# Latent attention: the first down projection blocks are loaded into other slots of the weight buffer

## The reference

```python
def mla_shared_kv(x, kv_in_g, w_dkv, kv_norm_g, w_uk, w_uv, cos, sin):
    ckv = rmsnorm(x, kv_in_g) @ w_dkv                       # 1024 -> 256 latent + 64 for the rotation
    latent = rmsnorm(ckv[..., :KV_LORA], kv_norm_g)
    k_rope = apply_rope(ckv[..., KV_LORA:], cos, sin)
    k_nope = (latent @ w_uk).reshape(b, s_len, MLA_HEADS, MLA_NOPE)
    v = (latent @ w_uv).reshape(b, s_len, MLA_HEADS, MLA_V)
    return k_nope, k_rope, v

# in mla_mixer: the query goes 1024 -> 768 -> 16 heads
q = (rmsnorm(h @ w_dq, q_norm_g) @ w_uq).reshape(b, s_len, MLA_HEADS, MLA_NOPE + MLA_ROPE)
```

## Time and profile before

| | |
|---|---|
| median of 3 executions | 3567.14 us |
| the three | 3567.11, 3567.14, 3570.8 us |
| profiled execution, its own time | 3568.08 us |
| its span | 3566.1 us |
| mean granted TensorE clock | 0.89 of full |
| PE busy | 2822.0 us, 79% |
| stretch from the end of the first feed-forward to the first scores | 3100.2 to 3175.0 us |

### The profile page before, as it was taken

One profiled execution on the slowest core, in us unless ns is written; L12 is line 12 of the kernel. 1 busy time (PEld: TensorE's weight loads), 2 busy tenths in 40 slices (PEclk: granted clock), 3 DMA queues, 4 the chain that ended last, 5 costly groups with the idle time before them and its releaser, 6 DMA issues.

```text
span 3566.1 us, 53144 instructions
## 1 busy us (share of the span) xinstructions
PE 2822.0 (79%) x19152; PEld 1680.4 (47%) x19152; DVE 2225.3 (62%) x5084; ACT 1393.8 (39%) x3587; POOL 854.8 (24%) x780
## 2 busy tenths in 40 slices
PE   4988898777776877786575977777767989999998
PEld 3877344233222433341144722222115879877997
DVE  5855766768777666678735467777763246523276
ACT  1213444434433334443334243334433247523275
POOL 0001433334343333433400133344440000000000
PEclk8988999999888998886677999999768999999999
DMA  8888999999999999999967699999994235433353
GB/s 328 309 313 347 419 420 420 420 420 408 421 420 394 420 414 415 413 412 387 361 224 257 256 421 421 421 414 421 416 413 159 112 124 194 156 118 109 118 192 127
DMA packets 177293, 1153.12 MB, mean 323 GB/s; under 512 B 21892, under 2 KB 30492, under 8 KB 43436
## 3 DMA queue, kind: packets, MB, share of 16 engines
q0 software_dynamic: 111632, 810.60, 55.4%
q1 hardware_dynamic: 59244, 321.94, 24.1%
q10 hardware_dynamic: 6192, 17.67, 1.3%
HBM read 1128.86 MB, written 21.27 MB: 323 GB/s over the span
## 4 chain that ended last, share of the span: by engine, by line
PE 40%; DMA 37%; DVE 11%; issue 6%; ACT 5%; POOL 1%; SPq 1%; ACTq 0%; DVEq 0%; POOLq 0%
DMA AR<-in_peer_uv,AR 32%; PE PS L2829 10%; PE PS L1308 6%; DVE AR L1496 4%; DMA W<-in_ada_w 3%; PE PS L1266 2%; PE PS L660 2%; PE PS L3327 2%; DVE AR L1471 2%; PE PS L2642 2%; PE PS L390 2%; PE PS L2060 2%; POOL AR L1520 1%; PE PS L521 1%; PE PS L1924 1%
## 5 line engine op out<-in xcount | busy, mean ns | idle before, releaser
L1308 PE MATMUL PS<-AR 64*64 64x512 f32 x6144 | 984.3, 720 | 498.7 <-ACT AR L1382 497.3
L1496 DVE CUSTOM_DVE_ANT_0 AR<-AR,H 128x1024 f32<-128x1024 f32 x768 | 938.4, 1224 | 540.8 <-DMA AR<-in_peer_uv,AR 534.6
L1520 POOL DMA_INDIRECT AR<-in_peer_uv,AR x768 | 850.1, 1107 | 1615.1 <-PE PS L1308 1156.8
L1308 PEld LDWEIGHTS PS<-AR 64*64 64x64 f32 x6144 | 180.1, 148 | 945.3 <-ACT AR L1382 830.0
L1377 ACT ACTIVATE SM<-SM 128x1 f32<-128x1 f32 x768 | 155.5, 202 | 1171.1 <-DVE SM L1496 1170.3
L1266 PE MATMUL PS<-HT,W 128*128 128x256 f32 x1280 | 427.8, 440 | 0.0
L1266 PEld LDWEIGHTS PS<-HT,W 128*128 128x128 f32 x1280 | 217.4, 200 | 424.7 <-issue 413.0
L1382 ACT ACTIVATE AR<-AR,SM 128x64 f32<-128x64 f32 x768 | 267.2, 348 | 25.2
L2829 PE MATMUL PS<-XP,WP 128*128 128x256 f32 x2112 | 258.4, 284 | 6.4 <-ACT AR L3003 3.5
L2829 PEld LDWEIGHTS PS<-XP,WP 128*128 128x128 f32 x2112 | 257.3, 193 | 8.7 <-DVE WP L3026 3.8
L1379 ACT ACTIVATE SM<-SM 128x1 f32<-128x1 f32 x768 | 226.3, 295 | 25.0
(11 more groups left out here) (402 smaller groups left out, 3394.7 us busy)
## 6 DMA issues: line engine op xcount, KB each, us to landing
W<-in_ada_w SPq DMA_DIRECT2D x48, 1024.0 KB, 8.0
W<-in_peer_w_q SPq DMA_DIRECT2D x44, 1024.0 KB, 9.5
W<-in_ffn_out SPq DMA_DIRECT2D x22, 1024.0 KB, 4.8
W<-in_ffn_gate SPq DMA_DIRECT2D x20, 1024.0 KB, 4.8
W<-in_ffn_val SPq DMA_DIRECT2D x20, 1024.0 KB
W<-in_cm_w_in SPq DMA_DIRECT2D x16, 1024.0 KB, 8.4
AR<-min_scr SPq DMA_DIRECT2D x16, 1024.0 KB, 6.7
AR<-in_peer_uv,AR POOLq DMA_INDIRECT x768, 15.7
```

Source lines behind the costliest of these rows:

```text
L1308: mm = pe.matmul(PS[c * self.HP:(c + 1) * self.HP, 4 + (u % 2) * 2 + half, :], self.DIAG[rows_, r % 4, :], self.UV[rows_, r % RING, D + c ...
L1496: v.tensor_tensor_reduce(rows_, rows_, H[:, self.tb(u), :], 1.0, 0.0, ALU.mult, ALU.add, self.ACTV[:, u % 2, k:k + 1]).then_inc(u_used.sem, 1)
L1520: g.indirect_dma_start(out=self.UV[:, r % RING, :], out_offset=None, in_=t["peer_uv"], in_offset=bass.IndirectOffsetOnAxis(ap=self.IDS[:, ...
```

## The change

The five down projection blocks keep their order, and PE, ACT and DVE do the same work in the same order. Only the slots change: latent block 2 -> 3, rotation block 3 -> 0, query blocks 0, 1, 2 -> 1, 2, 3. The bookings and all waits on these slots follow. The stage `mla`, whose `mla_ukv` block goes to slot 3, is not edited.

```diff
-            SLOT = dict(kv=2, rope=3, q=(0, 1, 2))
-            uw = take([1, 1, 2, 1])
+            uw = take([1, 1, 1, 2])
...
-                load(2, uw[2], t["mla_down"][QB])
-                load(3, uw[3], t["mla_down"][QB + 1])
-                load(0, uw[0], t["mla_down"][0])
-                load(1, uw[1], t["mla_down"][1])
-                load(2, uw[2] + 1, t["mla_down"][2])
+                load(3, uw[3], t["mla_down"][QB])
+                load(0, uw[0], t["mla_down"][QB + 1])
+                load(1, uw[1], t["mla_down"][0])
+                load(2, uw[2], t["mla_down"][1])
+                load(3, uw[3] + 1, t["mla_down"][2])
...
-                pe.wait_ge(w_full[2], (uw[2] + 1) * 16)
+                pe.wait_ge(w_full[3], (uw[3] + 1) * 16)
                 for tb in range(2):
-                    mm = rows_down(PS[:, 0, tb * COLS:(tb + 1) * COLS], tb, SEQ, 2)
-                mm.then_inc(w_used[2], 1)
+                    mm = rows_down(PS[:, 0, tb * COLS:(tb + 1) * COLS], tb, SEQ, 3)
+                mm.then_inc(w_used[3], 1)
                 turn_input(MLA_ROWS, 1)
-                pe.wait_ge(w_full[3], (uw[3] + 1) * 16)
+                pe.wait_ge(w_full[0], (uw[0] + 1) * 16)
...
-                mm.then_inc(w_used[3], 1)
+                mm.then_inc(w_used[0], 1)
                 pe.wait_ge(n_ht.sem, ht + T_MLA + 4)
                 for b in range(QB):
-                    pe.wait_ge(w_full[b], (uw[b] + (b == 2) + 1) * 16)
-                    mm = rows_down(PS[:, 2 + b // 2, b % 2 * COLS:(b % 2 + 1) * COLS], 0, 0, b)
+                    pe.wait_ge(w_full[1 + b], (uw[1 + b] + (b == 2) + 1) * 16)
+                    mm = rows_down(PS[:, 2 + b // 2, b % 2 * COLS:(b % 2 + 1) * COLS], 0, 0, 1 + b)
...
                 for b in range(QB):
-                    mm = rows_down(PS[:, 5 + b // 2, b % 2 * COLS:(b % 2 + 1) * COLS], 1, 0, b)
-                    mm.then_inc(w_used[b], 1)
+                    mm = rows_down(PS[:, 5 + b // 2, b % 2 * COLS:(b % 2 + 1) * COLS], 1, 0, 1 + b)
+                    mm.then_inc(w_used[1 + b], 1)
```

More of the change, by code:

```diff
@@ L3153, in pe_ @@
                 pe.wait_ge(sums_taken.sem, st)
-                pe.wait_ge(w_full[2], (uw[2] + 1) * 16)
+                pe.wait_ge(w_full[3], (uw[3] + 1) * 16)
                 for tb in range(2):
-                    mm = rows_down(PS[:, 0, tb * COLS:(tb + 1) * COLS], tb, SEQ, 2)
-                mm.then_inc(w_used[2], 1)
+                    mm = rows_down(PS[:, 0, tb * COLS:(tb + 1) * COLS], tb, SEQ, 3)
+                mm.then_inc(w_used[3], 1)
                 turn_input(MLA_ROWS, 1)
-                pe.wait_ge(w_full[3], (uw[3] + 1) * 16)
+                pe.wait_ge(w_full[0], (uw[0] + 1) * 16)
                 for half in range(2):
                     for k in range(KT):
-                        mm = pe.matmul(PS[:, 1, half * COLS:(half + 1) * COLS], W[:, 3, k * COLS + half * P:k * COLS + (half + 1) * P],
+                        mm = pe.matmul(PS[:, 1, half * COLS:(half + 1) * COLS], W[:, 0, k * COLS + half * P:k * COLS + (half + 1) * P],
                                        HT[:, k, SEQ:2 * SEQ], start=(k == 0), stop=(k == KT - 1))
-                mm.then_inc(w_used[3], 1)
+                mm.then_inc(w_used[0], 1)
                 pe.wait_ge(n_ht.sem, ht + T_MLA + 4)
                 for b in range(QB):
-                    pe.wait_ge(w_full[b], (uw[b] + (b == 2) + 1) * 16)
-                    mm = rows_down(PS[:, 2 + b // 2, b % 2 * COLS:(b % 2 + 1) * COLS], 0, 0, b)
+                    pe.wait_ge(w_full[1 + b], (uw[1 + b] + (b == 2) + 1) * 16)
+                    mm = rows_down(PS[:, 2 + b // 2, b % 2 * COLS:(b % 2 + 1) * COLS], 0, 0, 1 + b)
                 mm.then_inc(q_down, 1)
@@ L3211, in act_ @@
                 keep_input(T_MLA, 0)
-                a.wait_ge(w_used[2], uw[2] + 2)
+                a.wait_ge(w_used[3], uw[3] + 2)
                 a.copy(H[:, 2:4, 0:KVL], PS[:, 0, :].rearrange("p (t c) -> p t c", t=2)).then_inc(saved, 1)
@@ L3217, in act_ @@
                     root(2 + tb)
-                a.wait_ge(w_used[3], uw[3] + 2)
+                a.wait_ge(w_used[0], uw[0] + 2)
                 a.copy(RAW, PS[:, 1, :].rearrange("p (t c) -> p t c", t=2)).then_inc(saved, 1)
@@ L3221, in act_ @@
                     if tb:
-                        a.wait_ge(w_used[2], uw[2] + 3)
+                        a.wait_ge(w_used[3], uw[3] + 3)
                     else:
```

## The result

| | before | after |
|---|---|---|
| median of 20 executions | 3573.45 us | 3579.72 us |
| lowest to highest | 3567.11 to 3580.69 | 3570.84 to 3592.39 |
| profiled execution, its own time | 3568.08 us | 3581.24 us |
| its span | 3566.1 us | 3579.2 us |

The ratio of the changed kernel to the kernel before is 1.0021, 95% interval [1.0013, 1.0029]: slower by about 7.5 us (4.6 to 10.4). The two medians differ by 6.3 us and the two means by 7.5 us. The plain mean of the three is 1.0012, some 4.3 us; weighted by the width of their intervals it is 1.0014, some 5.2 us. The three executions of before that the prediction knew are among the seven lowest of its 20; the median of the 20 is 6.3 us higher.

A forecast was written before the change was run, and what follows sets the result against it. Around the edited stage the prediction saw PE work as the bound, with no entry load waited for. A 3.9 us wait for `mla_ukv` plus 1.7 us of half clock gave +5.6 on 3567.14: 3572.7 us, range 3569.0 to 3575.8.

The forecast's parts named there:

- The entry's loads were not waited for: Entry of the attention: ACT's copy, not a load, comes last before the latent product; earlier loads gain and cost 0.
- The wait for `mla_ukv`: Ahead of the first key product: slot 3 is freed only by the last query product, so PE starts 3.9 us later.
- Rival B: `mla_ukv` load slowed by three loads behind it, adding 1.7 us; 3574.4 to 3575.3 us, slower by over 0.2%; chance 0.23.
- The clock: Behind the new PE pause of 4.3 us: key products run at half clock, +1.7 us, between 0 and 2.6.
- The giveback: Later clock dip at 3176: may not come, -1.5 us, or a dip elsewhere may grow as much; taken as 0.
- Two things can shift the sum ... I take 0: Clock dip at 3176 may vanish (-1.5 us), or another may grow by as much; counted as 0 in the sum.
- nothing gives the time back: Chain behind the `mla_ukv` wait: PE work with short links, so the 3.9 us lost there stay lost.
- all behind is later by 5 to 6 us: Expected in the profile after: L3327 starts at about 3161.7 and everything behind it is 5 to 6 us later.
- if PE catches up in the rounds behind: Sign of a wrong prediction: PE regains the lost time in the rounds behind the new wait.
- C: Clock doesn't fall behind the wait, or the later dip goes away: +3.9 or +2.4 us, 3569.5 to 3571.0; chance 0.15.
- D: Entry does wait for its latent block and the change frees it: -2.3 us, 3564.8 us; chance 0.02.
- E: The change does nothing: first loads gain nothing and `mla_ukv` is not late; chance 0.01.

The follow-up runs named there:

- mean of the three: Three series of the changed kernel, each against the kernel before: ratios 1.0021, 1.0013 and 1.0002.
- the early loads alone: Against the kernel before: latent block to slot 0, rotation block stays in 3, query blocks to 1, 2, 0; ratio 1.0002.
- the kernel that fills the pause: Changed kernel plus 8 unused matmuls on PE during the new wait; ratios to the kernel before 1.0033 and 1.0012.
- the first series: Changed kernel against the kernel before, 20 executions: ratio 1.0021 [1.0013, 1.0029].
- the two others: Changed kernel timed again and a third time against the kernel before: ratios 1.0013 and 1.0002.
- the halves: Changed kernel with the first `mla_ukv` block loaded as two halves, key products waiting for the first only; ratio to the kernel before 1.0014.
- the larger wait: Changed kernel with `mla_ukv` issued behind the three query weight blocks, all after slot 3 is free; ratios to the kernel before 1.0054 and 1.0030.
- the late block: Third query block in slot 3, so `mla_ukv` is issued late; alone, other slots as in the kernel before, ratio to that kernel 1.0012.

## Why the prediction was right or wrong

**The entry's loads were not waited for: right.** The latent product starts 7.85 us behind the feed-forward, before 7.84, and the early loads alone give 113.65 us against 113.58. The three early loads took longer in their new place (a median of 11.8 us in the changed kernel's first profile, behind the gains), with room to spare, and the `ffn_out` block ahead of them still landed in 4.8 us.

**The wait for `mla_ukv`: right, 0.15 us too small.** +3.9 was forecast and +4.05 measured; the landing took 4.78, and PE began 0.25 us behind it where I had allowed 0.05. Rival B, in the form that loads issued behind it slow it down, is excluded by four profiles with 4.7 to 4.8 us. (The landing at which it decides should have read 4.8 + 7.1 - 5.6 = 6.3, not 6.4.) The fit of the Trainium skill ("DMA: Bandwidth & Descriptors", section "Anatomy of one DMA — SWDGE (gpsimd) path"), which is for another path, gives an estimate of 4.4; the row of the trace was nearer.

**The clock: right in place and size, +1.7 forecast, +1.69 measured.** That it was the clock and not the transfers is shown by the kernel that fills the pause.

**The giveback: wrong, a term of the sum put at 0 that measured -1.58.** I set the dip at the first scores at no change and named its loss of 1.5 us as a possible gain. It went away in all three profiles of the changed kernel. At the first scores the chain was later by 5.8 us against the feed-forward's end, as forecast (5.6); when the third round's query products start, by 4.25. So the term "Two things can shift the sum ... I take 0" should have been -1.6, and "nothing gives the time back" and "all behind is later by 5 to 6 us" were wrong with it. By its own words ("if PE catches up in the rounds behind") the working was wrong here.

**The absolute time: wrong, and this is the step that put it outside the range: the one from the difference to the median.** 3572.7 was 3567.14 + 5.6, and 3579.72 lies outside 3569.0 to 3575.8. The median of three executions was taken as the kernel's time with 0.5 us to each side, although the three already differed by 3.7. The 20 executions have their median at 3573.45, 6.3 us above the base, and the kernel before had medians of 3581.12, 3579.67 and 3573.89 in the later series (35, 17 and 35 executions, each series on another chip). With 5.6 us on top of 3573.45 it is 3579.1, 0.7 below what was measured. That closeness is luck: the forecast difference was 5.6 and the stretch has 4.25, while the first series happened to lie higher (+6.3 between the medians) than the two others. What varied was the work ahead, by 16.4 us over 13 profiles, and the rest, 352.2 to 352.4 in seven profiles, 352.8 in one (the halves) and 354.9 to 355.0 in five. I had given the stages behind the attention no term and no width at all.

**The rivals.** C (the dip behind the wait doesn't come) fell with its first half, and its second half happened. D (a gain) is excluded by the early loads alone. E (the change does nothing) is excluded by the stretch. On "slower by over 0.2%" the first series' 1.0021 lies at the bound, and the three together, 1.0012 to 1.0014, inside it.

What stays open: what makes the part ahead vary, and what decides between the two lengths of the rest. Both profiles of the larger wait and both of the filled pause have the long one, the changed kernel has it in one profile of three, and the two of the kernel before don't have it. Whether the change makes it more likely isn't shown; if it does, it costs more than the 4.25 us of the stretch. Nothing was tried on either.

## What to carry to other kernels

Before weight blocks change slots, look at what each slot is wanted for next: if its last reader in this stage now comes later, the next stage's block is issued later, and the one that had 17 us to spare may be the one that loses. Here the early loads had no part in the loss. Ask of each load not how long it takes but which signal came last before its reader; where that is an engine's copy, an earlier load gains nothing. Don't base an absolute forecast of 0.2% on the median of three executions, and judge such a change by a stretch of the trace whose length repeats.

## What the runs showed of the hardware

In the stretch, the dips of TensorE's clock repeated with the work. It kept its length within 0.25 us for each of the four programs with more than one profile (113.58 and 113.62; 117.71, 117.83 and 117.95; 124.43 and 124.44; 117.60 and 117.66), while it began up to 9.7 us apart for one program. A dip in it came or went only where the program changed or filled a pause ahead of it. Behind the stretch that held less well: the same changed kernel had a dip at the start of the group of 1176 records in one of three profiles. And work that no edit touched, some 147 us behind the stretch, changed with the wait ahead: its 96 records of L2829 took 13.1 us in the four profiles without the late block, 14.4 in eight of the nine with it, and 13.2 in the ninth, the one with the halves. Shortening a wait by 0.8 us made the stretch 2.1 us longer, and filling the pause with matmuls won 1.69 us and lost 1.56 at the next pause. A pause's price at half clock can't be read from its length alone: the same pause of 3.1 us ahead of the first scores cost 0, 1.6 or 3.0 us in these kernels.

The `mla_ukv` load issued first of four landed in 4.8 us, as alone; issued last of the four it took 9.4.
